# The first modulation of a two-block transformer kernel: rows or columns, and the place of x and ctx in the load queue

## The reference

```python
sc = jax.nn.silu(c)
scc = jax.nn.silu(c_ctx)
sh1x, s1x, g1x, sh2x, s2x, g2x = jnp.split(sc @ ada_w[l] + ada_b[l], 6, axis=-1)
sh1c, s1c, g1c, sh2c, s2c, g2c = jnp.split(scc @ ada_w[l] + ada_b[l], 6, axis=-1)
ux = x * (1.0 + s1x[:, None, :]) + sh1x[:, None, :]
uc = ctx * (1.0 + s1c) + sh1c
yx, yc = mixer_ab(ux, uc, ab_w_in[i], ...)      # begins with z @ w_in for z = ux, uc
```

## Time and profile before

| | |
|---|---|
| median of 3 runs | 2575.31 us (2575.0 to 2575.45) |
| the profiled execution's own time | 2568.04 us |
| its span | 2566.2 us |
| granted PE clock, mean | 0.953 |
| PE busy | 2226.7 us (87%) |
| PE weight loads busy | 1206.6 us (47%) |
| DVE busy | 865.3 us (34%) |
| ACT busy | 371.1 us (14%) |
| DMA | 698.21 MB, mean 272 GB/s |

### The profile page before, as it was taken

One profiled execution on the slowest core, in us unless ns is written; L12 is line 12 of the kernel. 1 busy time (PEld: TensorE's weight loads), 2 busy tenths in 40 slices (PEclk: granted clock), 3 DMA queues, 4 the chain that ended last, 5 costly groups with the idle time before them and its releaser, 6 DMA issues. The chain is left out here.

```text
span 2566.2 us, 35098 instructions
## 1 busy us (share of the span) xinstructions
PE 2226.7 (87%) x14019; PEld 1206.6 (47%) x14020; DVE 865.3 (34%) x1531; ACT 371.1 (14%) x623; POOL 140.3 (5%) x206
## 2 busy tenths in 40 slices
PE   6999978898888873996788888887799999989999
PEld 3344654443333332344442332222456777766776
DVE  2376566430000006667632200000543333492001
ACT  0000412111111111015211111111052000110000
POOL 0000010000000003010100000000210010000000
PEclk8999989899999996999889999999899999999999
DMA  8778521799999975781389999997433886434442
GB/s 291 271 266 325 191 64 65 303 423 423 422 423 423 422 328 182 280 307 74 133 343 421 423 422 423 422 422 324 159 131 124 313 306 237 159 113 148 148 149 81
DMA packets 176764, 698.21 MB, mean 272 GB/s; under 512 B 14085, under 2 KB 72325, under 8 KB 114096
## 3 DMA queue, kind: packets, MB, share of 16 engines
q1 hardware_dynamic: 158912, 622.76, 62.3%
q0 software_dynamic: 11968, 51.00, 5.5%
q10 hardware_dynamic: 5808, 23.42, 2.5%
HBM read 673.87 MB, written 22.20 MB: 271 GB/s over the span
## 5 line engine op out<-in xcount | busy, mean ns | idle before, releaser
L1579 PE MATMUL bank<-ring,arena 128*32 128x512 f32 (+1 forms) x3072 | 358.3, 615 | 78.2 <-DMA ring<-moe_w_up 51.2
L508 PE MATMUL bank<-ring,actT 128*128 128x512 f32 x768 | 336.9, 599 | 4.0 <-PEq L634 1.8
L2690 PE MATMUL bank<-actT,ring 128*128 128x256 f32 x1344 | 293.4, 379 | 0.0
L2690 PEld LDWEIGHTS bank<-actT,ring 128*128 128x128 f32 x1344 | 255.2, 190 | 42.3 <-issue 8.6
L1579 PEld LDWEIGHTS bank<-ring,arena 128*32 128x32 f32 x3072 | 100.5, 113 | 330.9 <-issue 329.3
L1596 PE MATMUL bank<-arena 128*32 128x512 f32 (+1 forms) x2048 | 226.6, 594 | 25.7 <-ACT arena L1670 24.7
L508 PEld LDWEIGHTS bank<-ring,actT 128*128 128x128 f32 x768 | 146.0, 192 | 194.7 <-issue 191.4
L1711 DVE TENSOR_TENSOR arena<-arena,bank 128x512 f32<-128x512 f32 x32 | 22.0, 688 | 612.8 <-ACT arena L1668 612.8
L583 DVE SCALAR_TENSOR_TENSOR arena<-ring,cols,arena 128x2048 f32<-128x2048 f32 x70 | 162.7, 2349 | 79.3 <-DMA ring<-ada_w 77.8
L2047 PEld LDWEIGHTS bank<-arena 128*128 128x128 bf16 x2448 | 141.0, 100 | 32.3 <-issue 26.8
L2702 PE MATMUL bank<-ring,arena 128*128 128x512 f32 x352 | 154.6, 593 | 0.0
(11 more groups left out here) (454 smaller groups left out, 2084.3 us busy)
## 6 DMA issues: line engine op xcount, KB each, us to landing
ring<-moe_w_gate SPq DMA_DIRECT2D x128, 1024.0 KB, 24.2
arena<-moe_w_down SPq DMA_DIRECT2D x128, 1024.0 KB, 21.7
ring<-ada_w SPq DMA_DIRECT2D x72, 1024.0 KB, 7.6
ring<-ffn_w SPq DMA_DIRECT2D x66, 1024.0 KB, 5.4
ring<-moe_w_up SPq DMA_DIRECT2D x64, 1024.0 KB, 23.7
actT<-moe_w_up SPq DMA_DIRECT2D x64, 1024.0 KB, 24.6
arena<-ada_w POOLq DMA_DIRECT2D x24, 1024.0 KB, 9.9
made_scratch<-arena ACTq DMA_DIRECT2D x32, 512.0 KB, 7.7
```

Of the source, the lines that this page charges most:

```text
L508: mm = nc.tensor.matmul(self.bank[g % 6][:, :], lhsT(m, k), halves[k // 4][:, k % 4, :], start=(k == 0), stop=(k == KT - 1))
L1579: mm = nc.tensor.matmul(bank[j // 2][Q * q:Q * q + Q, :], A(XS + P * kt + Q * q, Q), weights(j, own, q, k * DE, DE), start=(kt == 0), stop ...
L2690: mm = nc.tensor.matmul(bank[2 - 2 * (j % 2) + which][:, f * SEQ:(f + 1) * SEQ], w[:, k, f * P:(f + 1) * P], self.actT[:, k * T:k * T + SE ...
```

## The change

The first modulation is no longer made as rows. PE uses the four-band form of the hosting stage for it: for each piece, four matmuls with 32 columns of weights from `scx` (16 for c, 16 for c_ctx) write 512 columns each to a band of 32 partitions of bank 6. DVE adds the bias once over 512 columns, PE turns the result in four transposes, and two small DVE instructions store shifts and one plus scales as columns in `stat`: for each of x and ctx and each of the eight blocks k, one column of 128 values.

x and ctx are turned raw in the start stage: PE runs the 32 transposes between its units (the function `turn_x`), and ACT copies all eight groups to `actT`. At the start of the hosting stage DVE modulates `actT` in place, 16 instructions of 256 elements, each with one column of scale and one of shift (`modulate_turned`), and PE waits for each of the eight blocks in groups 0 and 2. The turning stage is gone.

x and ctx are issued by SP behind three pieces of the ring, no longer by ACT. ACT issues the identity's 128 columns of `k_misc` first and the other 512 last, and the bias as four loads of 32 partitions by 512 columns, between them.

```diff
 st_linear_hosting(..., turned=None):
                         for k in range(KT):
+                            if turned is not None and g in (0, 2):
+                                pe.wait_ge(turned.sem, turned.at(4 * g + k + 1))
                             mm = nc.tensor.matmul(self.bank[g % 6][:, :], lhsT(m, k), halves[k // 4][:, k % 4, :],
...
             def _(dve):
+                if turned is not None:
+                    self.modulate_turned(dve, turned)
...
 st_start, PE:
-                for k in range(KT):
-                    for n in range(4):
-                        mm = nc.tensor.matmul(self.bank[n][:, :], self.arena[:, WIDE + k * P:WIDE + (k + 1) * P],
-                                              sl[:, 0, 512 * n:512 * n + 512], start=(k == 0), stop=(k == KT - 1))
+                def unit(k):
+                    for j in range(4):
+                        mm = nc.tensor.matmul(bank[6][32 * j:32 * j + 32, :], self.scx[:, 32 * k:32 * k + 32],
+                                              sl[:, 0, 512 * j:512 * j + 512], start=(k == 0), stop=(k == KT - 1))
...
+                for k in range(5):
+                    unit(k)
+                pe.wait_ge(x_in.sem, x_in.at(32))
+                turn_x(0)
+                turn_x(1)
+                unit(5)
+                turn_x(2)
+                unit(6)
+                turn_x(3)
+                unit(7)
+                pe.wait_ge(sum_ready.sem, sum_ready.at(1))
+                for b in range(4):
+                    mm = nc.tensor.transpose(bank[7][:, b * P:(b + 1) * P], A(SUM + b * P, P), self.ident)
...
 SP:
+                self.feed(sp, 3)
+                half(0, "x")
+                half(1, "ctx")
                 self.feed(sp)
...
 ACT:
-                act.dma_start(self.misc[:, :], I["k_misc"]).then_inc(vec_in.up(16), 16)
-                act.dma_start(self.mod[:, 0:2048], rows_to_all(I["ada_b"][0][0:2048], 2048)).then_inc(bias_in.up(16), 16)
-                for s, n in enumerate(("x", "ctx")):
+                act.dma_start(self.misc[:, 0:P], I["k_misc"][:, 0:P]).then_inc(vec_in.up(16), 16)
+                for j in range(4):
...
+                act.dma_start(self.misc[:, P:5 * P], I["k_misc"][:, P:5 * P]).then_inc(bias_in.up(16), 16)
...
+                for n in range(8):
+                    act.wait_ge(x_turned.sem, x_turned.at(n + 1))
+                    nc.scalar.activation(self.put_mixed(n // 2, n % 2), dims(turn_to(n)[:, :], [P, 4], [1, P]), ACT.Copy).then_inc(raw_ready.up(), 1)
...
 DVE:
+                nc.vector.tensor_tensor(A(SUM, 512), bank[6][:, :], A(BIAS, 512), ALU.add).then_inc(sum_ready.up(), 1)
+                dve.wait_ge(sum_turned.sem, sum_turned.at(1))
+                nc.vector.tensor_scalar(columns(SHIFTS), by_block(0), 0.0, None, ALU.add)
+                nc.vector.tensor_scalar(columns(SCALES), by_block(64), 1.0, None, ALU.add)
...
+    def modulate_turned(self, dve, ready):
+        for v in range(2):
+            for k in range(KT):
+                xT = self.actT[:, k * T + v * SEQ:k * T + (v + 1) * SEQ]
+                self.nc.vector.tensor_scalar(xT, xT, self.stat[:, 432 + 8 * v + k:433 + 8 * v + k], self.stat[:, 416 + 8 * v + k:417 + 8 * v + k],
+                                             ALU.mult, ALU.add).then_inc(ready.up(), 1)
...
 mixer_ab:
-        self.st_transpose(O_t, 4, self.put_mixed, self.modulated(O_t, 0))
```

More of the change, by code:

```diff
@@ L429, in plan_ada, with st_linear_hosting @@
         self.plan(w[k * P:(k + 1) * P, 2048 * r:2048 * (r + 1)].rearrange("(k p) n -> p k n", p=P), 1, 2048)
-    def st_linear_hosting(self, lhsT, chunks, dest, rounds, sums, homes, pick, on_pe=(), lead=0, unmix=None, tables=None, beside=None):
+    def st_linear_hosting(self, lhsT, chunks, dest, rounds, sums, homes, pick, on_pe=(), lead=0, unmix=None, tables=None, beside=None, turned=None):
         nc, sm = self.nc, self.sem
@@ L747, in st_start @@
     def st_start(self):
-        nc, I = self.nc, self.I
+        nc, I, A, bank, sm = self.nc, self.I, self.A, self.bank, self.sem
         vecs = [I["c"], I["c_ctx"], I["c_2"], I["c_ctx_2"]]
-        WIDE, RAW = 20480, 21504
-        vec_in, bias_in, x_in = (self.sem[n] for n in ("vec_in", "bias_in", "x_in"))
+        RAW, BIAS, SUM = 21504, 4096, 4608
+        SHIFTS, SCALES = 416, 432
+        vec_in, bias_in, x_in, x_turned, raw_ready, sum_done, sum_ready, sum_turned = (sm[n] for n in (
+            "vec_in", "bias_in", "x_in", "z_turned", "zT_ready", "ada_done", "ada_added", "turned"))
+        turn_to = lambda n: bank[n % 6]
         with self.stage() as block:
@@ L768, in _, with turn_x @@
                     self.used += 1
+                def turn_x(t):
+                    for g in range(2):
+                        n = 2 * t + g
+                        if n >= 6:
+                            pe.wait_ge(raw_ready.sem, raw_ready.at(n - 5))
+                        for q in range(4):
+                            k = 4 * g + q
+                            mm = nc.tensor.transpose(turn_to(n)[:, q * P:(q + 1) * P], self.x_tile(t)[:, k * P:(k + 1) * P], self.ident)
+                        mm.then_inc(x_turned.up(), 1)
+                pe.wait_ge(vec_in.sem, vec_in.at(80))
+                nc.tensor.transpose(bank[7][:, 0:32], self.arena[0:32, RAW:RAW + P], self.ident[0:32, 0:32]).then_inc(self.pe_done.up(), 1)
+                pe.wait_ge(self.dve_done.sem, self.dve_done.at(1))
+                for k in range(5):
[11 more added lines that the diff above has]
+                    mm = nc.tensor.transpose(bank[7][:, b * P:(b + 1) * P], A(SUM + b * P, P), self.ident)
+                mm.then_inc(sum_turned.up(), 1)
             @block.sync
             def _(sp):
+                half = lambda s, n: sp.dma_start(self.xres[64 * s:64 * s + 64, :].rearrange("p (t d) -> p t d", t=4),
+                                                 I[n][0].rearrange("(t p) d -> p t d", p=64)).then_inc(x_in.up(16), 16)
+                self.feed(sp, 3)
+                half(0, "x")
+                half(1, "ctx")
                 self.feed(sp)
@@ L797, in _ @@
-                ins.then_inc(self.dve_done.up(), 1)
                 for v in range(4):
-                    nc.vector.tensor_copy(dims(self.scx[:, 256 * (v // 2) + 16 * (v % 2):], [32, KT], [1, 16]),
-                                          dims(self.cols[:, 8 * v:], [1, KT], [0, 16]))
-                dve.wait_ge(bias_in.sem, bias_in.at(16))
-                dve.wait_ge(self.pe_done.sem, self.pe_done.at(2))
-                for n in range(4):
-                    nc.vector.tensor_tensor(self.mod[:, 512 * n:512 * n + 512], self.bank[n][:, :],
-                                            self.mod[:, 512 * n:512 * n + 512], ALU.add)
@@ new lines, in _ @@
+                dve.wait_ge(sum_turned.sem, sum_turned.at(1))
+                by_block = lambda off: dims(bank[7][:, off:], [16, 2], [32, 2], [P, 4])
+                columns = lambda off: dims(self.stat[:, off:], [8, 2], [4, 2], [1, 4])
+                nc.vector.tensor_scalar(columns(SHIFTS), by_block(0), 0.0, None, ALU.add)
[6 more added lines that the diff above has]
+                                             ALU.mult, ALU.add).then_inc(ready.up(), 1)
@@ L853, in tables @@
                 (A(GT, 1152), I["k_gla"]), (mod[:, 0:4096], I["k_ret"])])
-        self.st_linear_hosting(lambda m, k: actT[:, k * T + m * P:k * T + m * P + P], AB_CHUNKS, dest, AB_ROUNDS, AB_SUMS, AB_HOMES, AB_PICK, AB_ON_PE, tables=tables)
+        self.st_linear_hosting(lambda m, k: actT[:, k * T + m * P:k * T + m * P + P], AB_CHUNKS, dest, AB_ROUNDS, AB_SUMS, AB_HOMES, AB_PICK, AB_ON_PE, tables=tables, turned=sm["zT_ready"])
         tables_in = self.params_in.total
```

22 lines of the change are left out of this document (11 added, 11 removed).

## The result

| | before | after |
|---|---|---|
| median | 2575.15 us (4 runs, 2574.19 to 2575.45) | 2554.0 us (4 runs, 2552.23 to 2559.39) |
| ratio of the runs | | 0.9925, 95% interval 0.9911 to 0.9938 |
| profiled execution | 2568.04 us | 2554.5 us |
| its span | 2566.2 us | 2552.7 us |
| granted PE clock, mean | 0.953 | 0.952 |

The changed kernel is faster: by the ratio 19.3 us (16.0 to 22.9) of the 2575.15. On two further chips the medians were 2573.37 and 2571.36 before, 2553.97 and 2554.25 after (ratios 0.9918, 0.9896 to 0.9941, and 0.9935, 0.9911 to 0.9959).

The account below looks back on a forecast made before the run. The bound was taken to be the start's chain up to the first hosting matmul. Moving that matmul from 58.7 to 40.0 us takes 18.7 off 2575.3, giving 2556.6 us; range 2550 to 2564.

Parts of the forecast that it names:

- its signs: Right: first hosting matmul at 40, no DMA wait up to 250 us; wrong: a later stage not 18.7 us earlier.
- the chain of the earlier trace: Start stage: first modulation, bias, modulating and turning, copies, until the first hosting matmul at 58.72 us; claimed to set the end.
- x and ctx in the stream: Start-stage loads: x and ctx, alone in their queue at 210 GB/s, take 10.0 us and are in at 21.5 us.
- Rival A: Start-stage loads: x and ctx move at the full rate, everything 5.1 us earlier, 2551.5 us; chance 0.13.
- Units and clock on PE: Start stage: PE's clock rises at 30.0 us; units then take 1.07 us, slow ones 2.14, the last ending at 36.9.
- B: Start stage: PE stays at 1.2 GHz until unit 7, 6.8 us later, 2563.4 us; chance 0.20.
- From the last unit to the first matmul: End of the start: bias add, transposes, small adds, barrier, one modulation and hand-overs take 3.1 us; first matmul at 40.0.
- the two pieces of ab_w_in follow in 5.0 us: 39.2 us: Weight stream: both ab_w_in pieces land behind piece 7 by 39.2 us, before the first hosting matmul at 40.0.
- C: Hosting stage: PE's clock is still high in group 0, 3.0 us more gained, 2553.6 us; chance 0.18.
- What could be late next: Hosting-stage stream: four pieces for hosted units and POOL's tables fit, cost 0; otherwise up to 9.8 us at stake.
- rival E: Hosting stage: the stream becomes its bound, costing 23.9 us at 265 GB/s, 2580.5 us; chance 0.04.
- The sum against the median: Whole kernel: the start's 18.7 us come off the median 2575.3, whose 7.3 us above the profiled execution stay the same.

Follow-up runs that it names:

- Experiments 1 and 2: 1: the old kernel with x and ctx issued by SP behind three pieces, 2573.91 us; 2: the changed kernel with them issued by ACT again, 2561.89 us.
- experiment 4: The changed kernel with x and ctx each loaded as two rows of 1024 to all 128 partitions, output differing; single time 2552.68 us, not compared.
- experiment 6: The changed kernel itself, unedited, run twice more on other chips: 2553.97 us and 2554.25 us.
- experiment 8: The changed kernel, with PE waiting for the second piece of ab_w_in only before the fifth matmul of group 0; 2555.12 us, ratio 0.9922.
- Experiment 9: The changed kernel with x and ctx turned from full-width loads, residual copy behind POOL's tables: 2561.68 us; also with the later wait for ab_w_in's second piece: 2563.54.

## Why the prediction was right

The forecast, 2556.6 us, stands against 2554.0 (2552.23 to 2559.39), inside the range, and of the cases the one forecast is the one that came. Not all its signs did: the start was at 41.86 instead of 40, PE waited 3.0 us for ab_w_in where it was to wait for no DMA, and the stage behind came 16.9 us earlier where anything but 18.7 was named as a sign of being wrong.

- **Where the gain is from.** Right: the chain of the earlier trace rows was the bound, and everything behind it moved with it. Experiments 1 and 2 split it, which the prediction did not: the parts are not a sum. Each bound hid the other.
- **x and ctx in the stream.** 10.0 us were taken from the row nearest to it; 9.7 were measured (experiment 4). Alone they moved at 216 GB/s where the sum had 210. Rival A (4.9) is out: one behind the other or in turn, the halves don't reach full rate. Side by side they were not tried.
- **Units and clock on PE.** The clock rose at 30.9 us, put at 30.0; the last unit ended at 37.3, put at 36.9. The 5.6 us that the prediction took from the earlier trace rows for the old rise are 6.0: a mean of 0.68 between 0.50 and 1.00 puts it at 54.6, not 54.3. From the first unit after the wait it was 5.4 here and 8.0 in experiment 6. A slow unit took 1.93 us, not 2.14. B is out: the clock was high in units 5 to 7 in all profiles of this kernel.
- **From the last unit to the first matmul.** 2.6 us to the first modulated column, which stood at 39.87; the sum had its use at 40.0. The terms of the 3.1 us add up to 3.0. In experiment 8, where the column was what PE waited for, it was 3.0 us from the last unit (37.09) to the first matmul (40.06).
- **The term mis-sized** is "the two pieces of ab_w_in follow in 5.0 us: 39.2 us". They had landed by 41.86, 2.7 us later, and they, not the columns, set the start, as experiment 8 shows. 1.0 us of it is piece 3, there at 25.45 instead of 24.4. That was not x and ctx: at full width, where the same sum with 4.9 us gives 19.3 (an estimate), piece 3 came 1.4 us late too, at 20.70. ACT's small loads were not in by 11.5 us, as the sum had it; 0.39 MB of them moved between 11.5 and 21.5. The other 1.6: from 25.45 to 41.86 SP's queue moved 6.72 MB, at 410 GB/s. The four pieces and two of ab_w_in are 6.29 MB of it. 1.1 us go to the 0.43 MB left, which can only be of pieces behind them, moved before the last of these had landed; 0.5 us is the rate:

```profile
25.45:33.00 7.55, 6.98 (x40) 2.77 (x40) 0.00 (x0) 2.03 (x4) 0.00 (x0) 0.64 1.02 424
34.00:39.00 5.00, 3.96 (x31) 1.64 (x29) 0.81 (x3) 2.06 (x4) 0.00 (x0) 1.00 1.03 383
```

The first stretch is pieces of ada_w, with rows of 8 KB; the second is ab_w_in, with rows of 2 KB. The prediction took 427 for the first and 423 for the second, the latter from the earlier trace rows, where it is ada_w that moves. The kernel before had shown the lower rate on the same two pieces:

```profile
39.00:44.00 5.00, 4.14 (x10) 1.50 (x8) 0.75 (x2) 0.00 (x0) 0.00 (x0) 1.00 1.07 394
```

The start stage gained 16.9 us, not 18.7.
- **Group 0's clock.** Forecast and C are both true of this kernel, in different executions: 10.11 and 9.98 us in two profiles, 7.11 in the third. C was a property of a run, not of the kernel.
- **What could be late next.** Right for the changed kernel. Experiment 9 is rival E's mechanism in small: at a start of 37 us and with 2 MB more, the stream was the bound of the hosting stage, for one chunk.
- **The sum against the median.** 18.7 was forecast and 16.9 came in the start; the medians moved by 17.1 to 21.2. The sum took the distance of the profiled execution from the median, 7.3 us, to be the same in both kernels; in the changed one it is -0.5, 0.2 and -0.2 us (median less profiled execution, three chips). So for the profiled execution the same sum gives 2549.3, and 2554.5 was measured. The forecast lies nearer to the median than its own mechanism earns, and that is luck: 16.9 us off the median would have been 2558.3.

## What to carry to other kernels

Two edits that each shorten one of two parallel chains (here PE's units and the arrival of the data that it turns) must be tried together: apart, one gave -1.7 and the other 8.7 us, together 16.9. When a start is brought forward, look at which load lands last in front of it and at the lead of the stream behind it; a load to half of the partitions cost about twice its bytes or more in every place tried here, so put it where nothing waits for the stream. Price a load by the rate of the same load in the old trace: ab_w_in had its own, lower rate there. For gains under some 5 us of 2575, medians of 4 to 12 runs do not tell; read the start of the stage that the edit touches, in more than one profile. That start was the same to 0.4 us in three profiles of one program, but a stage 200 us behind it differed by 2.7 and the medians' gain by 4.

## What the runs showed of the hardware beyond the expectation

- Loads to 64 partitions, one behind the other or in turn of 256 KB, held the stream at 226 to 250 GB/s (11 to 16 and 16 to 22 us); alone, from 17 to 21 us, they moved at 216 one behind the other and at 250 in turn; the same bytes to 128 partitions at 364 and 425. With ctx beside full-width pieces the two queues together moved 268.
- Pieces of ab_w_in, with rows of 2 KB, moved at 383 GB/s (34 to 39 us) and 394 before the change; pieces with rows of 8 KB at 424 just before. That the rows are the cause is not shown.
- The same program showed the PE clock at different levels in the same place: group 0 of the hosting stage took 10.11, 7.11 and 9.98 us in three profiles of the changed kernel, and 8.80, 8.72, 7.10 and 7.03 in variants of it.
- The gap of 37.3 to 41.9 us, in which PE has only four transposes, did not decide on that alone: in three profiles the clock fell in it twice and held once.
